# Seven half-block products in place of eight for most up projection groups of a Hymba layer

## The reference, cut to what matters

```python
def channel_mlp(x, g, w_up, w_down):
    h = rmsnorm(x, g)                                      # 1024 features
    u = jnp.maximum(jnp.einsum('btd,df->btf', h, w_up), 0)  # w_up: 1024 x 4096
    return jnp.einsum('btf,fd->btd', u * u, w_down)         # w_down: 4096 x 1024
```

## Time and profile before

| | us |
|---|---|
| median of 3 runs | 2390.11 |
| lowest, highest | 2389.84, 2390.34 |
| span of the profiled execution, first to last instruction | 2388.1 |
| TensorE busy / VectorE / ScalarE / GpSimd | 2362.5 / 1377.4 / 963.6 / 79.3 |
| granted TensorE clock, mean over the span | 0.999 |

### The profile page before, as it was taken

One profiled execution on the slowest core, in us unless ns is written; L12 is line 12 of the kernel. 1 busy time (PEld: TensorE's weight loads), 2 busy tenths in 40 slices (PEclk: granted clock), 3 DMA queues, 4 the chain that ended last, 5 costly groups with the idle time before them and its releaser, 6 DMA issues.

```text
span 2388.1 us, 33521 instructions
## 1 busy us (share of the span) xinstructions
PE 2362.5 (99%) x13086; PEld 2016.6 (84%) x13086; DVE 1377.4 (58%) x3162; ACT 963.6 (40%) x2050; POOL 79.3 (3%) x136
## 2 busy tenths in 40 slices
PE   9999999999999999999999999999999999999998
PEld 8988888888897888888998788888888879889996
DVE  4478554456378654455456854554656785555555
ACT  4445433334345533334333543333434454333332
POOL 3000000000000000000000210000010000000000
PEclk9999999999999999999999999999999999999999
DMA  6212323333511223324421233223444122222221
GB/s 193 79 45 90 96 97 98 96 109 106 170 55 54 81 96 97 96 90 132 147 80 37 68 99 97 90 96 97 133 124 133 45 67 88 77 84 80 88 80 66
DMA packets 175402, 224.28 MB, mean 94 GB/s; under 512 B 15107, under 2 KB 126308, under 8 KB 175228
## 3 DMA queue, kind: packets, MB, share of 16 engines
q1 hardware_dynamic: 162636, 192.63, 25.8%
q10 hardware_dynamic: 6448, 19.40, 2.3%
q0 software_dynamic: 6160, 10.11, 1.6%
HBM read 210.72 MB, written 12.60 MB: 94 GB/s over the span
## 4 chain that ended last, share of the span: by engine, by line
PE 95%; DVE 4%; ACT 1%; issue 1%; DVEq 0%; ACTq 0%
PE ps L2066 28%; PE ps L2068 28%; PE ps L2067 27%; PE ps L2077 2%; PE ps L2207 2%; PE ps L2187 1%; PE ps L2196 1%; PE ps L2253 1%; PE ps L2256 1%; DVE w_lo L1177 1%; PE ps L2103 0%; PE ps L2596 0%; PE ps L2115 0%; PE ps L2232 0%; DVE w_lo L1173 0%
## 5 line engine op out<-in xcount | busy, mean ns | idle before, releaser
L2068 PE MATMUL ps<-a_hi,w_lo 128*128 128x512 f32 (+2 forms) x1672 | 583.9, 349 | 0.0
L2066 PE MATMUL ps<-a_hi,w_hi 128*128 128x512 f32 (+2 forms) x1672 | 582.1, 348 | 0.6 <-DVE a_lo L1181 0.2
L2067 PE MATMUL ps<-a_lo,w_hi 128*128 128x512 f32 (+2 forms) x1672 | 582.0, 348 | 0.0
L702 ACT ACTIVATE w_hi<-w_raw,gains 128x256 fp32r<-128x256 f32 (+1 forms) x576 | 253.2, 521 | 411.3 <-PE ps L2068 290.6
L2066 PE MATMUL ps<-w_hi,u_all 128*128 128x512 f32 x1024 | 403.8, 394 | 0.0
L2068 PE MATMUL ps<-w_hi,u_all 128*128 128x512 f32 x1024 | 403.8, 394 | 0.0
L2067 PE MATMUL ps<-w_lo,u_all 128*128 128x512 f32 x1024 | 401.3, 392 | 0.0
L2066 PEld LDWEIGHTS ps<-a_hi,w_hi 128*128 128x128 f32 x1672 | 315.8, 189 | 43.1 <-DVE a_lo L1181 1.4
L2067 PEld LDWEIGHTS ps<-a_lo,w_hi 128*128 128x128 f32 x1672 | 314.0, 188 | 40.9
L2068 PEld LDWEIGHTS ps<-a_hi,w_lo 128*128 128x128 f32 x1672 | 314.2, 188 | 39.4
L1181 DVE TENSOR_TENSOR x<-x,ps 128x512 f32<-128x512 f32 (+1 forms) x288 | 196.5, 686 | 259.8 <-PE ps L2068 241.9
(11 more groups left out here) (378 smaller groups left out, 2336.1 us busy)
## 6 DMA issues: line engine op xcount, KB each, us to landing
w_raw<-in_w_up_dram SPq DMA_DIRECT2D x128, 512.0 KB, 3.7
w_raw<-in_w_down_dram SPq DMA_DIRECT2D x128, 512.0 KB, 3.5
w_raw<-in_w_out_dram SPq DMA_DIRECT2D x32, 512.0 KB, 3.5
w_raw<-in_w_in_dram SPq DMA_DIRECT2D x24, 580.0 KB, 4.9
w_raw<-in_w_in_dram SPq DMA_DIRECT2D x22, 512.0 KB, 3.7
w_raw<-in_w_in_dram SPq DMA_DIRECT2D x32, 256.0 KB, 2.9
wide<-in_x_prompt_dram ACTq DMA_DIRECT2D x12, 512.0 KB, 4.6
x<-in_x_prompt_dram ACTq DMA_DIRECT2D x9, 512.0 KB, 6.2
```

Source lines behind the costliest of these rows:

```text
L702: ins = eng.activation(w_hi[b][:, k * n:(k + 1) * n][:, s], src[:, s], ACT.Copy, scale=gain[:, a:a + 1])
L2066: eng.matmul(out, lh, rh, start=(k == ks[0]), stop=False)
L2067: eng.matmul(out, lh, rl, start=False, stop=False)
L2068: ins = eng.matmul(out, ll, rh, start=False, stop=(k == last))
```

## The change

14 of the 16 up units of a quarter (all but the first two, which stay as they were) are computed by seven products of half blocks instead of eight. A unit's weights are cut into two halves of the features (κ) and two of the rows (φ), the activations into two halves of the features and two of the tokens. Each product has 4 blocks x 3 matmuls, 256 tokens wide; in the last quarter four of the seven are 320 wide.

- GpSimd forms four sums of weight blocks per unit, S1 = A21 + A22, S2 = S1 - A11, S4 = A12 - S2, S3 = A11 - A21, each 128 x 512, into `PT`. ScalarE and VectorE split seven forms of 128 x 512 (`high_form`, `low_form`) instead of two pieces.
- VectorE forms four sums of activation blocks once per quarter (`x_sums`), 128 x 1024 each; ScalarE and VectorE split them too.
- The results are put together by ScalarE (`take_copy`) and VectorE (`take_sum`, seven steps), then ReLU, square and high part are three steps of ScalarE (`square_up`) and the remainder one of VectorE.
- The norm gain is multiplied into the activations by VectorE (`take_tile`) in place of the weights, so `high_tile` now waits for VectorE and reads SBUF. The MLP's weight forms live in a ring of 9 slots (`RING`).
- `bias` shares its memory with the MLP and is fetched again by GpSimd each quarter (8 DMAs). The ahead tiles 0 and 1 use `PT`.
- In VectorE's `step` the four calls for the next quarter now stand at the end of the step.

The diff, cut to its core:

```diff
+            def all_sums(q):
+                pool.wait_ge(xf_ok.sem, xf_ok.at(q, 2 * len(tokens_of(q == QM)[1])))
...
+                    for k in range(2):
+                        landed(pool, q, 2 * u + k)
+                    if at:
+                        pool.wait_ge(f_high.sem, f_high.at(q, 7 * at))
+                        pool.wait_ge(f_split.sem, f_split.at(q, 7 * at))
+                    pool.tensor_tensor(src("S1"), src("A21"), src("A22"), ALU.add).then_inc(f_sum.sem, 1)
+                    pool.wait_ge(f_sum.sem, f_sum.at(q, 4 * at + 1))
+                    pool.tensor_tensor(src("S2"), src("S1"), src("A11"), ALU.subtract).then_inc(f_sum.sem, 1)
+                    pool.wait_ge(f_sum.sem, f_sum.at(q, 4 * at + 2))
+                    pool.tensor_tensor(src("S4"), src("A12"), src("S2"), ALU.subtract).then_inc(f_sum.sem, 1)
+                    pool.tensor_tensor(src("S3"), src("A11"), src("A21"), ALU.subtract).then_inc(f_sum.sem, 1)
...
@@ scalar: step
+                    if seven(u) is not None:
...
+                        if before is not None:
+                            square_up(before, 1)
+                        take_copy(u)
+                        next_part(0)
+                        next_part(1)
+                        next_part(2)
+                        next_part(3)
+                        square_up(u, 0)
...
@@ vector: ahead of the MLP
                     norm_tile(q, NT, 1)
+                    take_tile(q, NT, 0)
                     low_tile(q, NT, 0)
                     op_at(2, 3)
                     split_vec(eng, q, U_M, 0)
+                    take_tile(q, NT, 1)
                     low_tile(q, NT, 1)
                     split_vec(eng, q, U_M, 1)
...
                 norm_tile(q, NT, NT - 2)
                 norm_tile(q, NT, NT - 1)
+                take_tile(q, NT, NT - 2)
                 low_tile(q, NT, NT - 2)
+                take_tile(q, NT, NT - 1)
                 low_tile(q, NT, NT - 1)
...
@@ vector: step
+                    if before is not None:
+                        take_sum(before, 6)
+                    if seven(u) is not None:
...
+                        if before is not None:
+                            low_sum(before, 0)
+                        next_part(1)
+                        take_sum(u, 0)
+                        if before is not None:
+                            low_sum(before, 1)
+                        next_part(2)
+                        take_sum(u, 1)
+                        take_sum(u, 2)
+                        next_part(3)
+                        take_sum(u, 3)
+                        next_part(4)
+                        take_sum(u, 4)
+                        take_sum(u, 5)
+                        next_part(5)
...
-                    if u == UNITS - 4 and not last:
-                        scale_ahead(q + 1, 0)
...
                     else:
                         eng.wait_ge(dn_read.sem, dn_read.at(q, 2 * NT * c))
...
+                        next_part(5)
+                    if u == UNITS - 4 and not last:
+                        scale_ahead(q + 1, 0)
+                    if u == UNITS - 3 and not last:
+                        take_ahead(q + 1, 0)
+                    if u == UNITS - 2 and not last:
+                        scale_ahead(q + 1, 1)
+                    if u == UNITS - 1 and not last:
+                        take_ahead(q + 1, 1)
...
@@ tensor
+                def product(u, f, w, right):
+                    eng.wait_ge(f_split.sem, f_split.at(q, 7 * seven(u) + f + 1))
+                    hi, lo = form_at(w_hi_all, u, f), form_at(w_lo_all, u, f)
+                    out = product_bank(seven(u), f)[:, 0:w]
+                    for k in range(4):
+                        rh, rl = right(k, w)
+                        eng.matmul(out, hi[:, k, :], rh, start=(k == 0), stop=False)
+                        eng.matmul(out, hi[:, k, :], rl, start=False, stop=False)
+                        ins = eng.matmul(out, lo[:, k, :], rh, start=False, stop=(k == 3))
+                    ins.then_inc(m_done.sem, 1)
...
+                    bank_free(0, 2)
+                    product(u, 0, ws, b11)
+                    bank_free(1, 4)
+                    product(u, 1, ws, b21)
+                    bank_free(2, 6)
...
+                    product(u, 2, ws, turned_part("T1"))
+                    bank_free(3, 7)
...
+                    product(u, 3, HT, turned_part("T2"))
+                    eng.wait_ge(cp_ok.sem, cp_ok.at(q, at + 1))
+                    product(u, 4, HT, b22)
+                    eng.wait_ge(c_add.sem, c_add.at(q, 7 * at + 1))
...
+                    product(u, 5, HT, turned_part("T3"))
+                    eng.wait_ge(c_add.sem, c_add.at(q, 7 * at + 3))
+                    product(u, 6, ws, turned_part("T4"))
```

More of the change, by code:

```diff
@@ L56 @@
 WMAX = KT * TMW
+FORM = 512
+T_ALL = 6424
+T_SECOND = 4376
+RING = 9
+N_PLAIN = 2
 def unit_of(u):
@@ L71, in dmas_of, with mlp_unit, seven, plain_before @@
     return 3 if u == U_T else 1
+MLP_HEAD = [("U", 0)]
+MLP_BODY = 3
+MLP_TAIL = [("U", NC - 1), ("D", NC - 2), ("D", NC - 1)]
+MLP_ORDER = MLP_HEAD + [(k, c) for i in range(MLP_BODY) for k, c in (("U", 2 * i + 1), ("D", 2 * i), ("U", 2 * i + 2), ("D", 2 * i + 1))] + MLP_TAIL
+def mlp_unit(u):
+    kind, c = MLP_ORDER[(u - U_M) // 2]
+    return kind, c, (u - U_M) % 2
+def seven(u):
+    if not U_M <= u < UNITS:
+        return None
+    kind, c, half = mlp_unit(u)
+    return 2 * c + half - N_PLAIN if kind == "U" and 2 * c + half >= N_PLAIN else None
+N_SEVEN = sum(seven(u) is not None for u in range(UNITS))
+FORMS_OF = "A11 A12 S1 S2 S4 S3 A22".split()
+def plain_before(u):
+    return 2 * sum(seven(v) is None for v in range(u))
+PLAIN = plain_before(UNITS)
+def ring_at(u):
+    return sum(4 if seven(v) is None else 7 for v in range(U_M, u))
+RING_USER = [(u, f) for u in range(U_M, UNITS) for f in range(4 if seven(u) is None else 7)]
 def raw_of(q, p):
@@ L471, in u_views, with mlp_walk, piece_view @@
                     [u_all[:, n + b * 4 * lo:n + (b + 1) * 4 * lo].rearrange("p (k t) -> p k t", k=4) for b in range(2)])
-        def mlp_walk(eng, q, last, step):
-            u = U_M
-            for kind, c in kinds:
-                for half in range(2):
-                    step(kind, c, half, u, 0)
-                    u += 1
+        def mlp_walk(step):
+            for u in range(U_M, UNITS):
+                step(u, *mlp_unit(u))
+        def piece_view(q, u, k):
+            return raw[raw_of(q, 2 * u + k)][:, 0:4 * 256].rearrange("p (a b) -> p a b", b=256)
@@ L1988, in step @@
-                            eng.wait_ge(u_sq.sem, u_sq.at(q, o + 1))
-                            low(l, o, t, off, w)
-                            if n == NN - 1 and not end and u != U_M:
-                                split_vec(eng, nq, nu, 1, i)
+                            low_up(u, t, off, w, half * 2 * NN + n + 1)
+                        if half:
+                            for n in (3, 4, 5):
+                                next_part(n)
+                        else:
+                            t_low_part(2)
@@ L2561, in quarter, with t_at @@
                     eng.wait_ge(op_read.sem, op_read.at(q, 4 * NT))
-                def step(kind, c, half, u, i):
+                ws = staging(last)[0]
+                t_hi, t_lo = ({name: parts[i] for name, parts in t_forms(last).items()} for i in range(2))
+                def t_at(name, k, w):
+                    if name == "T2":
+                        return t_hi[name][:, k // 2, k % 2, 0:w], t_lo[name][:, k, 0:w]
+                    return t_hi[name][:, k, 0:w], t_lo[name][:, k, 0:w]
```

673 lines of the change are left out of this document (475 added, 198 removed).

## The result

The changed kernel takes 2431.11 us (median of 4 runs, 2429.35 to 2434.68) against 2390.23 us for the kernel before beside it: ratio 1.0173, 95% interval 1.0158 to 1.0187. It is slower by 41 us. The prediction said 2365 us, with a range up to 2398. The profiled span is 2430.0 us, 41.9 more than before.

What follows compares the result with a forecast made beforehand. The prediction took TensorE, busy 99% of the span, to bound the kernel. Its terms summed to 77 - 32 - 12 - 8 = 25 us won, 2365 us against 2390.1; own range 2348 to 2382, widened to 2338 to 2398.

Steps and rivals of the forecast that it cites:

- Term 1: Changed U units: 84 narrower matmuls in place of 48, at 0.116 us each, save 77 us (67 to 87).
- Term 2: Change of quarter: VectorE's moved calls make TensorE wait 2.8, 2.8 and 5.0 us, three times; 32 us lost (28 to 34).
- Term 3: Ahead of the MLP: VectorE's added take_tile instructions delay U0 and its second halves; 12 us lost (6 to 18).
- Term 4: First changed unit of each quarter: extra VectorE and ScalarE work, 2 us per quarter, 8 us lost (0 to 12).
- what was costed at nothing: VectorE's and ScalarE's work in changed units, later w_up loads, bias fetches and GpSimd's sums: all hidden, 0 us.
- the tightest place: Second U unit of a pair: GpSimd's sums cost nothing up to 2.3 us each; 1.2 us expected.
- Rival A: GpSimd's sums decide in every pair of U units from 2.3 us per sum; at 3.0 us, 2443 us; chance 0.10.
- Rival B: VectorE's remainders and GpSimd's sums hold each other up; at worst 53 us, more likely some 15 us; chance 0.15.
- Rivals C and D: C: the change-of-quarter loss doesn't come, 2333 us; D: seven narrow products no shorter than eight, 2442 us; chance 0.05 each.
- a rule that the prediction itself quoted: VectorE instructions with two SBUF inputs and GpSimd instructions that read SBUF exclude each other for a whole instruction.

Runs made afterwards that it cites:

- e3: Changed kernel with GpSimd's four sums per unit replaced by memsets, which leaves the weight sums out of the computation: 2391.86 us.
- b1: Kernel before, with only VectorE's four calls for the next quarter moved to the end of their step: 2436.85 us.
- e4: Changed kernel with TensorE's three pauses per change of quarter filled with 22, 22 and 40 matmuls whose result nobody reads: 2418.15 us.
- e1: Changed kernel with VectorE's four calls for the next quarter put back ahead of the four adds of their D unit: 2398.98 us.
- e5: e1 with ScalarE issuing the loads of the next quarter's first two token tiles earlier, in unit UNITS - 5: 2389.43 us.
- e6: e1 with GpSimd fetching bias again only after the last but one chunk's down products: 2391.42 us.
- e11: e8 with every sum of GpSimd made twice, one behind the other: 2533.83 us.
- e8: e7 with the second and third sum of results ahead of two remainders in each quarter's first changed unit: 2363.01 us.
- e9: e8 with 16 filler matmuls in TensorE's wait ahead of U0's second halves, first three quarters: 2360.37 us.
- e2: Changed kernel with VectorE's first sum of results ahead of the next D piece's remainder in a pair's second U unit: 2399.90 us.
- e7: Changed kernel with all three repairs, e1, e2 and e5: 2363.74 us.

## Why the prediction was wrong

**Term 1, the products** (77 us, 67 to 87). At the bare pace of e3 a pair saves 22.24 - 19.84 = 2.40 us, 2.54 in the last quarter: 7 x 3 x 2.40 + 7 x 2.54 = 68 us. The low end held. The step that was off is the mean of two paces: the new forms have 0.118, nearly the slower of rows 4. The load of weights did overlap, as the prediction argued: 168 loads and matmuls take 19.84 us.

**Term 2, the change of quarter** (32 us). Its mechanism was right, to about 0.1 us per pause; its size was not. b1 gives 47 us for it alone. The step that failed is adding up pauses as if TensorE went on at full clock behind them: 16 of the 47 us are the low clock, 1.5 of these behind no pause, and e4 took 13 back by filler alone. The mean clock of 0.999 in the kernel before told only that it had no such pause. Beside it a second lateness was overlooked, the load of the next tiles and the fetch of `bias` costed at nothing (e1, e5, e6); in the changed kernel the calls cover it.

**Term 3, ahead of the MLP** (12 us). U0 starts 0.9 to 1.6 us later against the last O products (5.2 in all). Its second halves come 10.57 us behind U0's start in place of 8.74 in the first three quarters and 10.86 in place of 7.78 in the last, 8.6 in all. Together 14 us, inside the 6 to 18.

**Term 4 and what was costed at nothing.** This is the second failure, and the larger one. The stalls beyond the bare pace are 1.28 us per pair in the first three quarters and 0.4 to 0.6 in the last, 26 us in all, where 0 stood, and 21 us in the first pairs, where 8 stood. The step was the search for the tightest place: I took the bank that product 3 of the next unit needs, at 13.9 us, as the deadline of a unit's last sum. The chain through `square_up`, `take_copy`, the D split and `low_sum` to `take_sum(u, 0)` ends in product 5 and is earlier. From the last sum's end (311.82) to the end of `take_sum(u, 0)` (317.61) it lasts 5.8 us. Product 4 ends near 316.3, so the last sum had to start by 316.3 - 5.8 - 0.4 = 310.1, 10.8 us into the pair; it started at 12.1. The 1.3 us between are the stall. Of the 21 us in the first pairs e3 takes 13 away: the sums of activation blocks run beside GpSimd's there. The 8 that are left are what the term forecast.

**Rival A** had too high a threshold, 2.3 us where e11 gives an estimate of 1.4; the duration of a sum (1.2 forecast, 1.29 alone, 1.50 as it runs) was close. **Rival B** is what happened in kind: the two engines take turns. Its worst case was 53 us; e3, which takes the reads away, wins 39. Chance 0.15 was too low beside a rule that the prediction itself quoted. No rival put B beside a larger term 2, and both came. **Rivals C and D** didn't come.

Sum of what was measured: -68 + 49 + 14 + 26 + 21 = 42 us, against 41.9 between the spans. The forecast was 67 us better: 9 of them are term 1, 17 term 2, 2 term 3, 13 term 4 and 26 the stalls in the pairs that were costed at nothing. The range was also narrower than its terms: with all four bounds at their ends it is 2337 to 2387, where the text has 2348 to 2382. The measured time lies outside of both.

## What to carry to other kernels

Cost a new pause of the bounding engine twice: its own length, and the low clock behind it (here mostly 1.5 us behind 2.7, and 1.9 to 2.3 behind 4.9). For each result that the bounding engine waits for, walk back through every engine's order, not only through the buffer that it frees, and put the instruction that it waits for ahead of those that nobody wants yet. When work goes to GpSimd, look at what VectorE does with two SBUF inputs in the same stretch, and check small moved calls first: here the four of them cost 47 us in b1, more than the 32 us that the pairs won, and with the order mended and the loads early the same algorithm is 1.1% faster than the kernel before (e8), 1.3% with filler (e9).

## What the runs showed of the hardware

- A pause of 2.7 us lowered TensorE's granted clock to 0.5 in five of six cases in the changed kernel's trace, one of 4.9 us in all nine cases of the traces of the changed kernel, e2 and b1. An idle time of 1.97 us did it three times in e7 and never in e2. 16 transposes then take 3.2 us in place of 1.7, and 512-column matmuls start 0.43 us apart in place of 0.23.
- The clock also fell with no pause, behind a run of small matmuls: 0.57 from 1824 to 1828 us of the changed kernel, 0.66 from 1751 to 1761 us of e8.
- Filler matmuls of 128 columns kept the clock at 1.00 in place of 0.50 where TensorE waited anyway, and the kernel went from 2431 to 2418 us.
- GpSimd adds two blocks of 128x512 in 1.29 us when alone. Beside VectorE's two-input instructions it takes 1.6 to 2.2, and VectorE's of 128x512 up to 1.78 in place of 0.68. A memset of the same block takes 0.53 us, and beside it VectorE's of 128x512 have a mean of 0.68.
- With eight fetches of 128 KB each on another queue beside it, a load of two tiles of 512 KB took 8.3 us from issue to landing (median, e1), without them 5.5 (e6).
- 168 matmuls of 256 columns, each with its own load of a 128x128 block, took 19.84 us (e3), 0.118 us each.
